# Transposes of a transformer's first block moved inside its projections, and latents turned before they are scaled

## The reference, cut to what matters

```python
for l in range(DEPTH):                       # 2
    h = rmsnorm(x, g_mix[l])
    dq, dk, dv, c_q, c_kv_kr, xq, gate_logits = jnp.split(h @ w_in[l], split_idx, axis=-1)
    y_diff = diff_attention(dq, dk, dv, ...) @ w_diff_o[l]       # 8 heads, two softmax maps each
    y_mla  = latent_attention(c_q, c_kv_kr, ...) @ w_mla_o[l]
    mem_n  = rmsnorm(mem, mem_gain[l])
    y_mem  = memory_cross_attention(xq, mem_n, ...) @ w_cross_o[l]
    gates  = jax.nn.sigmoid((gate_logits + b_gate[l]).reshape(B, S, N_BRANCHES, D))
    merged = gates[:, :, 0] * y_diff + gates[:, :, 1] * y_mla + gates[:, :, 2] * y_mem
    x = x + merged @ w_out[l]
    x = x + jnp.square(jax.nn.relu(rmsnorm(x, g_mlp[l]) @ w_mlp1[l])) @ w_mlp2[l]

# in latent_attention; rmsnorm(c, g) = c * (row factor) * g
q  = (rmsnorm(c_q, qa_gain) @ w_qb).reshape(...)       # c_q: 384 wide
kv = (rmsnorm(c_kv, kva_gain) @ w_kvb).reshape(...)    # c_kv: 256 wide, k_rope: 32 wide
```

## Time and profile before

| | us |
|---|---|
| median of 3 runs | 2975.85 (2973.08 to 2976.11) |
| the profiled execution | 2971.55 |
| its span, first to last instruction | 2969.7 |
| PE busy in the span | 2740.5 (92%) |
| POOL, DVE, ACT busy | 1868.5, 1081.9, 746.6 |
| mean granted PE clock, share of full | 0.967 |

### The profile page before, as it was taken

One profiled execution on the slowest core, in us unless ns is written; L12 is line 12 of the kernel. 1 busy time (PEld: TensorE's weight loads), 2 busy tenths in 40 slices (PEclk: granted clock), 3 DMA queues, 4 the chain that ended last, 5 costly groups with the idle time before them and its releaser, 6 DMA issues. The chain is left out here.

```text
span 2969.7 us, 38883 instructions
## 1 busy us (share of the span) xinstructions
PE 2740.5 (92%) x14264; PEld 2252.2 (76%) x14268; DVE 1081.9 (36%) x1902; ACT 746.6 (25%) x1455; POOL 1868.5 (63%) x1562
## 2 busy tenths in 40 slices
PE   6898999999999997899999999999998998989997
PEld 4687777778888886678777778888887976778765
DVE  4354364211210113245183320310102486427773
ACT  3241464200220201331365110120111114212250
POOL 5547321788898995647420788898896772366604
PEclk9999999999999998999999999999998999999998
DMA  4322100233233333322100233223233430042202
GB/s 123 85 61 77 41 8 12 81 93 96 89 96 97 95 96 81 96 77 74 52 8 1 72 88 96 90 93 99 93 99 79 94 79 29 29 89 76 76 1 71
DMA packets 159285, 214.80 MB, mean 72 GB/s; under 512 B 51696, under 2 KB 69360, under 8 KB 159088
## 3 DMA queue, kind: packets, MB, share of 16 engines
q1 hardware_dynamic: 120336, 207.27, 24.1%
q10 hardware_dynamic: 38752, 4.95, 1.3%
HBM read 210.06 MB, written 2.10 MB: 71 GB/s over the span
## 5 line engine op out<-in xcount | busy, mean ns | idle before, releaser
L292 POOL TENSOR_TENSOR weight_parts<-weight_ring,zero 128x512 fp32r<-128x512 f32 (+3 forms) x736 | 791.2, 1075 | 775.8 <-PE ps L377 396.9
L295 POOL TENSOR_TENSOR weight_parts<-weight_ring,weight_parts 128x512 fp32r<-128x512 f32 (+4 forms) x804 | 1062.1, 1321 | 155.3 <-ACT weight_parts L303 97.0
L379 PE MATMUL ps<-h_feature_major_high,weight_parts 128*128 128x512 f32 x2304 | 584.8, 394 | 13.1 <-ACT arena L1486 5.3
L379 PEld LDWEIGHTS ps<-h_feature_major_high,weight_parts 128*128 128x128 f32 x2304 | 431.0, 189 | 117.1 <-POOL weight_parts L292 10.0
L377 PE MATMUL ps<-weight_parts,h_feature_major_high 128*128 128x512 f32 (+3 forms) x1920 | 438.7, 369 | 39.1 <-DVE h_feature_major_low L1687 9.1
L377 PEld LDWEIGHTS ps<-weight_parts,h_feature_major_high 128*128 128x128 f32 x1920 | 344.3, 193 | 94.4 <-issue 18.8
L379 PE MATMUL ps<-h_feature_major_low,weight_parts 128*128 128x512 f32 x1152 | 310.0, 391 | 0.0
L377 PE MATMUL ps<-weight_parts,ut_high 128*128 128x512 f32 x1024 | 254.7, 390 | 0.0
L379 PEld LDWEIGHTS ps<-h_feature_major_low,weight_parts 128*128 128x128 f32 x1152 | 217.5, 189 | 45.8
L377 PE MATMUL ps<-weight_parts,h_feature_major_low 128*128 128x512 f32 (+3 forms) x960 | 234.7, 368 | 0.0
L377 PEld LDWEIGHTS ps<-weight_parts,ut_high 128*128 128x128 f32 x1024 | 191.6, 188 | 42.2 <-POOL weight_parts L295 1.7
(11 more groups left out here) (245 smaller groups left out, 2848.8 us busy)
## 6 DMA issues: line engine op xcount, KB each, us to landing
weight_ring<-in_w_in SPq DMA_DIRECT2D x272, 256.0 KB, 2.7
weight_ring<-in_w_mlp SPq DMA_DIRECT2D x256, 256.0 KB, 2.7
weight_ring<-in_w_out SPq DMA_DIRECT2D x64, 256.0 KB, 2.6
weight_ring<-in_w_mem_kv SPq DMA_DIRECT2D x32, 256.0 KB, 2.9
weight_ring<-in_w_diff_o SPq DMA_DIRECT2D x32, 256.0 KB, 2.6
weight_ring<-in_w_in SPq DMA_DIRECT2D x32, 170.0 KB, 2.7
weight_ring<-in_w_in SPq DMA_DIRECT2D x32, 168.0 KB, 2.2
...
```

The costliest lines, as they stand in the source:

```text
L292: self.nc.gpsimd.tensor_tensor(high, raw, self.m["zero"][:].broadcast_to([P, raw.shape[1]]), ALU.add).then_inc(self.s["slab_high"], 1)
L295: self.nc.gpsimd.tensor_tensor(low, raw, high.bitcast(F32), ALU.subtract).then_inc(self.s["slab_split"], 1)
L379: last = self.nc.tensor.matmul(banks[:, t, :], w[:, cut], h, **ends)
```

## The change

A transposing group can now be *inside* a projection: it takes the half that its host doesn't use, and it stands in the list ahead of its host. `begin` waits for the last group on the same half, which it now remembers per half.

- `xq_t` goes in front of `dq1`'s slab 4, `mk_t` in front of its slab 6; ACT's order for `dq0` becomes that of the other two, with the two sets of copies between its high parts.
- `lat_t0` and `lat_t1` go in front of `dv0`'s slabs 2 and 5. The latents are turned as they come from the projection, from `probs` and `probs_key_major`; DVE writes their low parts first and sums the squares afterwards. The eight scaling passes are gone; the row factor is the `scale` of ACT's copies of `qb0`, `qb1`, `kvb0` and `kvb1`, for which `qb0` and `qb1` are copied in four tiles.
- `d_t0` to `d_t2` go in front of `dv1`'s slabs 2, 4 and 6, `d_t3` in front of `qb0`'s slab 1.
- `o_t0` to `o_t2` go in front of `gate01`'s slabs 2, 4 and 6, `o_t3` in front of `y00`'s slab 2; `y01` now comes before `gate02`.
- `h2_t1`, which was inside `up00` already, uses the general way.

```diff
@@ -72,6 +72,9 @@
     def __init__(self, groups):
         self.groups = groups
         self.names = list(groups)
+        hosts = [n for n in self.names if "inside" not in groups[n]]
+        self.half = {n: k % 2 for k, n in enumerate(hosts)}
+        self.half |= {n: 1 - self.half[groups[n]["inside"]] for n in self.names if n not in self.half}
...
+        k = self.order.half[name]
...
     def begin(self, pe, name):
-        i = self.order.index(name)
-        assert i == len(self.done), name
-        self.done.append(name)
-        if i >= 2:
-            self.emptied(pe, self.order.names[i - 2])
-        if name in self.first_wait:
-            pe.wait_ge(*self.first_wait[name])
+        half = self.order.half[name]
+        if self.last[half]:
+            self.emptied(pe, self.last[half])
+        self.last[half] = name
+        if half in self.first_wait:
+            pe.wait_ge(*self.first_wait.pop(half))
...
-        "dq0": tok(w_in, 0, W512, by="dve"), "xq_t": turned, "mk_t": turned,
+        "dq0": tok(w_in, 0, W512, by="dve"), "xq_t": dict(turned, inside="dq1"), "mk_t": dict(turned, inside="dq1"),
...
-        "dv0": tok(w_in, C_DV, W512), "lat_t0": parts, "lat_t1": parts,
-        "dv1": tok(w_in, C_DV + W512, W512), "d_t0": turned, "d_t1": turned, "d_t2": turned, "d_t3": turned,
+        "lat_t0": dict(parts, inside="dv0"), "lat_t1": dict(parts, inside="dv0"), "dv0": tok(w_in, C_DV, W512),
+        "d_t0": dict(turned, inside="dv1"), "d_t1": dict(turned, inside="dv1"), "d_t2": dict(turned, inside="dv1"),
+        "dv1": tok(w_in, C_DV + W512, W512), "d_t3": dict(turned, inside="qb0"),
...
-    merge_order = ["gate00", "o_t0", "o_t1", "gate01", "y00", "o_t2", "o_t3", "gate02", "y01", "y02"]
+    merge_order = ["gate00", "o_t0", "o_t1", "o_t2", "gate01", "o_t3", "y00", "y01", "gate02", "y02"]
+    hosts = {"o_t0": "gate01", "o_t1": "gate01", "o_t2": "gate01", "o_t3": "y00"}
...
-            groups[name] = parts
+            groups[name] = dict(parts, inside=hosts[name])
...
-    groups["h2_t1"] = parts
+    groups["h2_t1"] = dict(parts, inside="up00")
...
-    lat = view(arena, 8192, TT, LATW)
+    latq = view(m["probs"][:].rearrange("p a b n -> p (a b n)"), 0, TT, QLORA)
+    latkv = view(m["probs_t"][:].rearrange("p a b n -> p (a b n)"), 0, TT, LATW - QLORA)
...
             L.project(pe, "dq0", ht)
-            pe.wait_ge(s["cross_normed"], 1)
-            L.turn(pe, "xq_t", [(h, t * P, xq[:, t, h * P:(h + 1) * P]) for h in range(CH) for t in range(TT)])
-            L.turn(pe, "mk_t", [(h, t * P, mk[:, t, h * P:(h + 1) * P]) for h in range(CH) for t in range(2)])
-            for name in ("dq1", "dk0"):
-                L.project(pe, name, ht)
+            def turn_xq():
+                pe.wait_ge(s["cross_normed"], 1)
+                L.turn(pe, "xq_t", [(h, t * P, xq[:, t, h * P:(h + 1) * P]) for h in range(CH) for t in range(TT)])
+            def turn_mk():
+                L.turn(pe, "mk_t", [(h, t * P, mk[:, t, h * P:(h + 1) * P]) for h in range(CH) for t in range(2)])
+            def turn_latent(k):
+                L.emptied(pe, "lat1")
+                chunks = range(4) if k == 0 else (4,)
+                lat_chunk = lambda t, c: latq[:, t, c * P:(c + 1) * P] if c < 3 else latkv[:, t, (c - 3) * P:(c - 2) * P]
+                L.turn(pe, f"lat_t{k}", [(c % 4, t * P, lat_chunk(t, c)) for c in chunks for t in range(TT)])
+            def turn_diff(k):
+                pe.wait_ge(s["diff_roped"], 1)
+                L.turn(pe, f"d_t{k}", [(c, t * P, qk[:, t, (4 * k + c) * P:(4 * k + c + 1) * P]) for c in range(4) for t in range(TT)])
+            L.project(pe, "dq1", ht, {4: turn_xq, 6: turn_mk})
+            L.project(pe, "dk0", ht)
             L.attend(pe, A, 0, U1, ("dk1", ht), ("lat0", ht))
-            for name in ("lat1", "dv0"):
-                L.project(pe, name, ht)
-            pe.wait_ge(s["latent_normed"], 1)
-            L.turn(pe, "lat_t0", [(c, t * P, lat[:, t, c * P:(c + 1) * P]) for c in range(4) for t in range(TT)])
-            L.turn(pe, "lat_t1", [(0, t * P, lat[:, t, 4 * P:5 * P]) for t in range(TT)])
-            L.project(pe, "dv1", ht)
-            pe.wait_ge(s["diff_roped"], 1)
-            for k in range(4):
-                L.turn(pe, f"d_t{k}", [(c, t * P, qk[:, t, (4 * k + c) * P:(4 * k + c + 1) * P]) for c in range(4) for t in range(TT)])
+            L.project(pe, "lat1", ht)
+            L.project(pe, "dv0", ht, {2: lambda: turn_latent(0), 5: lambda: turn_latent(1)})
+            L.project(pe, "dv1", ht, {2 + 2 * k: lambda k=k: turn_diff(k) for k in range(3)})
             L.emptied(pe, "lat_t1")
-            for name in ("qb0", "qb1", "kvb0", "kvb1"):
+            L.project(pe, "qb0", latt, {1: lambda: turn_diff(3)})
+            for name in ("qb1", "kvb0", "kvb1"):
                 L.project(pe, name, latt)
...
+            def turn_out(k):
+                if k == 0:
+                    pe.wait_ge(s["outs_ready"], 1)
+                src, off = ((od, 0), (od, 4 * P), (om, 0), (oc, 0))[k]
+                L.turn(pe, f"o_t{k}", [(c, t * P, src[:, t, off + c * P:off + (c + 1) * P]) for c in range(4) for t in range(TT)])
+            made = {"0": lambda: L.emptied(pe, "o_t1"), "1": lambda: L.emptied(pe, "o_t2"),
+                    "2": lambda: L.emptied(pe, "o_t3")}
+            woven = {"gate01": {2: lambda: turn_out(0), 4: lambda: turn_out(1), 6: lambda: turn_out(2)}, "y00": {0: made["0"], 2: lambda: turn_out(3)}}
             for name in merge_order[1:]:
                 if name[0] == "g":
-                    L.project(pe, name, ht)
+                    L.project(pe, name, ht, woven.get(name))
                 elif name[0] == "y":
-                    L.project(pe, name, ot, {0: lambda b=int(name[-1]): L.emptied(pe, ("o_t1", "o_t2", "o_t3")[b])})
-                else:
-                    k = int(name[-1])
-                    if k == 0:
-                        pe.wait_ge(s["outs_ready"], 1)
-                    src, off = ((od, 0), (od, 4 * P), (om, 0), (oc, 0))[k]
-                    L.turn(pe, name, [(c, t * P, src[:, t, off + c * P:off + (c + 1) * P]) for c in range(4) for t in range(TT)])
+                    L.project(pe, name, ot, woven.get(name) or {0: made[name[-1]]})
...
             def turn_right():
-                L.emptied(pe, "wo1")
+                L.begin(pe, "h2_t1")
                 turn_x(L.banks("h2_t1"), W512).then_inc(s["banks_full"], 1)
-                L.done += ["h2_t1", "up00"]
...
-                        L.project(pe, "up00", ht, {2: turn_right, 4: lambda: L.emptied(pe, "h2_t1")},
-                                  lambda pe, name: pe.wait_ge(s["left_split"], 1))
+                        L.project(pe, "up00", ht, {0: lambda: pe.wait_ge(s["left_split"], 1), 2: turn_right,
+                                                   4: lambda: L.emptied(pe, "h2_t1")})
...
-                if g == 0:
-                    full(act, name)
-                    square(name)
-                    scaled("xq_t", [(xqt[:, h, :], h, P, SEQ, cqg) for h in range(CH)])
-                    scaled("mk_t", [(mkt[:, h, :], h, P, MEM, ckg) for h in range(CH)])
-                    highs(0, 3)
-                else:
-                    highs(0, 2)
-                    full(act, name)
-                    square(name)
-                    highs(2, 3)
+                highs(0, 2)
+                full(act, name)
+                square(name)
+                highs(2, 3)
                 roots(st_d[:, :, 8 * g:8 * (g + 1)])
                 highs(3, 6)
+                if g == 0:
+                    scaled("xq_t", [(xqt[:, h, :], h, P, SEQ, cqg) for h in range(CH)])
                 if following == "dk1":
                     A.exp(0)
                     A.exp(1)
                 highs(6, KC)
+                if g == 0:
+                    scaled("mk_t", [(mkt[:, h, :], h, P, MEM, ckg) for h in range(CH)])
...
-            empty("lat0", lat[:, :, 0:LATW // 2], width=LATW // 2)
-            empty("lat1", lat[:, :, LATW // 2:], width=LATW // 2)
-            roots(st_lat)
-            empty("dv0", dv[:, :, 0:W512])
+            empty("lat0", latq[:, :, 0:LATW // 2], width=LATW // 2)
+            full(act, "lat1")
+            rest = QLORA - LATW // 2
+            a.activation(latq[:, :, LATW // 2:], L.banks("lat1")[:, :, 0:rest], ACT.Copy)
+            a.activation(latkv, L.banks("lat1")[:, :, rest:LATW // 2], ACT.Copy).then_inc(emptied, 1)
             L.write_high("lat_t0", split["lat_t0"])
             L.write_high("lat_t1", split["lat_t1"])
+            empty("dv0", dv[:, :, 0:W512])
+            roots(st_lat)
+            for k in range(3):
+                empty(f"d_t{k}", qkt[:, 4 * k:4 * k + 4, :])
             empty("dv1", dv[:, :, W512:])
-            for k in range(4):
-                empty(f"d_t{k}", qkt[:, 4 * k:4 * k + 4, :])
+            empty("d_t3", qkt[:, 12:16, :])
             qflat = view(arena, 0, TT, MH * MQK)
```

(26 more changed lines are left out.)

17 lines of the change are left out of this document (6 added, 11 removed).

## The result

The changed kernel takes **2926.11 us** (median of 4 runs, 2923.81 to 2931.21) beside 2974.47 for the kernel before on the same chip (4 runs, 2970.43 to 2976.11): ratio 0.984, interval 0.9827 to 0.9852. It is faster by 48.4 us; the forecast was 56.5. The profiled execution of after is its slowest, 2931.21 us with a span of 2929.0, so a difference of two spans (40.7) understates the gain. I compare stretches of layer 0 instead.

A forecast was written before the change was run, and what follows sets the result against it. TensorE, busy 92%, bounds the kernel; its idle and low-clock time can be saved. Per layer 13.47 + 9.32 + 0.57 + 4.63 + 1.45 - 1.2 = 28.2 us, 56.5 in two, from 2975.85 gives 2919.4 us; range 2911 to 2938.

The forecast's parts named there:

- the likeliest case: The forecast itself: 56.5 us saved in two layers, 2919.4 us, with nothing new waiting; chance 0.72.
- rival 1: One new wait, most likely for dq0's banks in dq1: 5.5 us a layer, 2930 us; two places 2941; chance 0.20.
- D: o_t0 to o_t3 moved into gate01 and y00: 4.63 and 1.45 us a layer saved, before the cost of returns.
- A: xq_t and mk_t moved into dq1: 13.47 us a layer saved, if nothing new waits.
- the margin of 0.96 us: At xq_t's turn in dq1: dq0's last product ends 9.92 us in, the turn comes 10.88 us in.
- B and C: Latents into dv0: 9.32 us a layer saved; d_t0 to d_t3 into dv1 and qb0: 0.57 us.
- Nobody waits: cost 0: Row factor in eight copies, qb0 and qb1 copied in four passes: cost 0, at worst 1.1 us a layer.
- Untouched: GpSimd's splits: GpSimd's weight splits stay at 1.08 + 1.32 = 2.40 us per slab against TensorE's 2.72; no change charged.
- New cost: First pass behind transposes takes 1.17 us instead of 1.07; twelve returns to matmuls add 1.2 us a layer.
- the unit price of 0.116: Charged us per TensorE transpose, from 32 in a row taking 3.71 us.
- Rival 2: Woven transposes cool the clock: half clock and 2.49 us ramps, 50 us a layer, 3019 us; chance 0.02.
- Rival 3: Saved time is met again as waits for split weights: half remains, 2948 us, or none, 2976; chance 0.06.

## Why the prediction was right, and where it was off

Time and direction were right (2926.11 in a range of 2911 to 2938, faster), and the likeliest case was not the one that happened: this is rival 1's event, one new wait, in a place and for an engine that rival 1 did not name. That the time still lies in the range is due to the range, which was drawn through rival 1, and to transposes that were cheaper than charged; the mechanism forecast for D was wrong.

- **A, 13.47 a layer: right.** 13.58 came (12.61 in layer 1, where before took 100.92), with dq0's banks back 9.92 us in and the margin of 0.96 us shown by moving the turn.
- **B and C, 9.89: right but for the copies.** 8.31 came, 9.31 in layer 1. In layer 0, 0.71 of what is missing is the longer wait for kvb1; the other 0.9 is less than what this stretch varies by. The step that failed is "Nobody waits: cost 0". It priced the split of qb0 and qb1 and passed over kvb0 and kvb1, whose last copy is what the diff attention waits for (L985 stood in the waits of before, 3.5 us in two). The Trainium skill ("ScalarE: Activation LUTs", What ACT_TABLE_LOAD costs) gives some 93 ns for each operand that is a pointer; the copies' 0.09 us agree. An estimate from that page's figure, eight copies at 0.093, would have been 0.74 us.
- **D, 5.7 with its returns: wrong by 4.3.** The step that failed is "Untouched: GpSimd's splits". They take 1.08 and 1.32 us on the page's mean, and one of them took 5.22 in the same place before, hidden by the very wait that D removes. A mean over 736 passes hid it. The prediction asked what covers each edit, and did not ask what the removed wait had covered.
- **New cost, 1.2: right; the unit price of 0.116 was too high.** The first pass behind each woven turn takes 1.00 to 1.02 us instead of 0.91, 0.1 for each of the twelve returns. But the price came from the modelled length of a row of 32, 3.71 us. From one start to the next, ten woven turns of sixteen take 1.66 or 1.67 us, mk_t 0.79 and lat_t1 0.35: 17.8 us for the 172 transposes, where 0.116 each is 20.0. That gave back 2.2 us a layer, 4.3 in all.
- **Rival 1** had the form and the size (a miss of 3 us and a fall of the clock, 5.5 a layer, 2930): measured 3.62 us and 5.5 us a layer, 2926. Its cause was another: VectorE was on time, and what it did beside GpSimd made GpSimd late. I had written that VectorE's passes stretch beside the splits; it is also the other way round.
- **Rival 2** fell: clock 1.00 through 32 woven transposes. **Rival 3**, what is saved met again as waits for split weights, named the releaser: D's new wait is one for a high part. Its size fell: all waits for high parts sum to 18.6 us before (13.8 and 4.8) and 29.0 after (17.0 and 12.0), 10.4 more and not half of 56, and 7.2 of them are the two held splits; with these repaired or gone the sum is 19.2 to 22.5.
- The sum closes within the spread: 56.5 - 11 (D's pass, two layers) - 1.4 (kvb1's copies) + 4.3 (cheaper transposes) = 48.4, against 48.4 and 49.5 measured. Without the 11 it is 59.4, and the kernel without the multiplication saves 60.5. With the pass in four 6 of the 11 come back, so 54.4; that kernel saves 60.4, and the shorter latent attention in its trace, 2.6 and 3.0 us, is about what lies between. The closeness is partly luck: the sum leaves out the longer diff attention, 2.18 us in layer 0 and 0.95 in layer 1.

What stays open: how long the lower clock lasts behind a wait of an attention. It shows in two places. From the first scores of the diff attention to those of the latent attention, layer 0 took 112.06 us before and 114.24, 114.15, 114.26 and 114.25 in four kernels with the 2.48 us wait, but 112.3 to 112.5 in four others with the same wait, and 112.5 to 112.9 in the three with 1.16. The four matmuls behind the 2.48 us wait took 2.08 us in layer 0 of the kernel after and 1.13 in layer 1. And the latent attention took 46.8 to 47.0 us or 49.5 to 49.9 up to gate00, behind the same 1.94 us. So after such a wait the clock recovers sooner in some executions than in others, and no run here tells what decides; the spread of the medians (some 3 us) is of this size.

## What to carry to other kernels

When a change takes out a wait, read what every other engine does during that wait, row by row and not by the mean of its line: anything late there becomes the next wait. A long VectorE pass with both inputs in SBUF stopped GpSimd until its end; cut it into pieces if GpSimd feeds the bottleneck (here 3.0 of 5.5 us came back), and leave it whole if the bottleneck waits for the pass itself. Small turns of transposes may stand between the slabs of a projection at their own price and 0.1 us for the return, if their inputs are ready and their bank half is free. Before an experiment's gain is put down to its edit, compare the stretch that the edit touches: here about half of a gain of 11 us lay in an attention that nothing had changed.
